# First feed-forward of a two-block transformer kernel: 512-column products with halves added on VectorE, and a re-timed plan

## The chip, the cores and the metric

One core of one Trainium2 chip runs the whole program. The metric is device time in microseconds (us) for one execution. Below, TensorE, VectorE, ScalarE and GpSimd appear in rows of the profile as PE, DVE, ACT and POOL; SPq is the queue from which the weight loads are issued.

## What is computed

Two transformer blocks, one after the other, on one sequence of 256 tokens of width 1024, in float32. The first block has a mixer of three branches (a forgetting attention, a gated delta rule, a stick-breaking attention), a memory cross-attention, and the feed-forward that this change is about. The second block has a feed-forward, a mixer (blockwise attention with 8 heads beside a pooling mixer), a memory cross-attention and another feed-forward. The feed-forward of the first block has a causal convolution of three taps over the tokens between its two products:

```
def conv_ffn(h, w_up, conv_w, conv_b, w_down):
    u = causal_dwconv(h @ w_up, conv_w) + conv_b
    a, b = jnp.split(u, 2, axis=-1)
    return (jax.nn.silu(a) * b) @ w_down
```

`w_up` is 1024 x 5632, `w_down` 2816 x 1024. The other two feed-forwards are `(silu(h @ w_gate) * (h @ w_up)) @ w_down` of the same sizes, without convolution.

## The kernel before

**Chunks.** All weights stream through once in chunks of 1 MB, on a ring of three slots (`RING = 3`). A chunk is loaded to `raw`, ScalarE rounds it to the high part `whi` (step `hi`, line 1443), and VectorE forms the low part `wlo = raw - whi` (step `lo`, line 1693). The activations are split in the same way (`xh` and `xl`, side by side in `xhl`), and each product is the sum of three: high by high, high by low, low by high. `hi` of a chunk waits until the product three chunks before has ended; the load of a chunk waits for the `lo` three chunks before. `hi` and `lo` are issued two chunks ahead (`LEAD = 2`).

**Kinds of chunk.** Kind A (line 1131) multiplies in three matmuls of 256 columns for each of 8 k-blocks and 2 column blocks: 48 matmuls, and all three sums land in the same 256 columns of one PSUM bank. Kind W (lines 1139 and 1142) multiplies `whi` once with `xh` and `xl` joined (512 columns) and `wlo` with `xh` (256 columns): 32 matmuls, two banks, and the two halves of each bank have to be added afterwards, which VectorE does with a TENSOR_REDUCE (steps `add`, `ga`, `ua`). Kinds V (line 1158) and R (line 1170) have the activations as the stationary side; R is the kind of the down and output products, with 4 banks, 24 matmuls a chunk.

**Order of the work.** `build_plan` writes one list of steps; each engine runs its own steps of the list strictly in that order. For each chunk `c`, `mm(c)` puts down `hi(c+2)` and `lo(c+2)`, then what was left over in the list `late`, then the product in two halves, and then the steps that read it. Between the halves and between chunks `hook` lets "links" of side chains in (the heads of the attentions, the norms): a link goes in when the planner's own clock, advanced by the cost table `ROUGH`, says that its input has been done for long enough (`fits`, with `EARLY` and `EARLY_LONG`). The real waits are semaphore waits; the planner's clock only decides the place of the link in the order. Side chains are not present in the feed-forwards.

**First feed-forward, before.** 11 pairs of chunks (gate `g`, up `u`), both of kind A. After the pair's second product: `ca(i)` on ScalarE (line 1644: last tap times the product plus bias, four instructions, read from the banks), `cd(i)` on VectorE (line 1950: the two other taps, eight instructions, read from the banks). In the next pair's first chunk, behind `hi` and `lo` of that chunk: `fs` (ScalarE, silu), `fm` (VectorE, line 1984), `fh` (ScalarE, line 1662), `fl` (VectorE, line 1988). So VectorE's order in a pair is lo, fm, fl, lo, cd, and ScalarE's hi, fs, fh, hi, ca. 11 chunks of `w_down` (kind R) follow. The other two feed-forwards have kind W and steps `ga(i)` after the gate product and `ua(i)` after the up product (lines 1975 and 1980).

**Second block's mixer, before.** The four pooling windows are made by GpSimd (`pl_win`), multiplied by TensorE (`pl_mm`, line 1417) in the middle of the fourth chunk before `w_out_2`, into banks 2 and 3, and read by `pl_h` (ScalarE) and `pl_l` (VectorE). The first R chunk of `w_out_2` waits for the last readers of all four of its banks before its first matmul.

## Time and profile before

| | |
|---|---|
| median of 3 runs | 1211.7 us (1209.04 to 1212.9) |
| the profiled execution | 1205.77 us |
| its span | 1204.0 us |
| granted TensorE clock, mean | 0.991 of full |
| TensorE busy | 1156.5 us, 96% |
| VectorE busy | 811.0 us, 67% |
| ScalarE busy | 614.9 us, 51% |
| GpSimd busy | 80.9 us, 7% |
| chain that ended last | TensorE 85%, VectorE 7%, ScalarE 4% |
| products of the first feed-forward's up stage | from about 443 to 569.7 us of the span |

The profile is of one execution on the hardware. The busy time of an engine counts its instructions alone; a matmul's end is modelled and overlaps the next one, so that the distance between starts tells the pace and not the duration of one. "Idle before" with a releaser is how long an engine stood before an instruction and what ended the wait.

### The profile page before, as it was taken

The numbers are of one execution on the slowest core, as the hardware profiler recorded it, in microseconds if no ns is written. First come the engines' busy times: TensorE is split into PE (matmuls) and PEld (weight loads), VectorE is DVE, ScalarE is ACT, GpSimd is POOL, SyncE is SP. The second block draws the span as 40 slices with busy tenths as digits, with TensorE's granted clock in tenths as the row PEclk, the third lists the DMA queues.
The fourth block names the chain that finished last, engine by engine and source line by source line (L and its number), as shares of the span: only waits on it lengthen the run. The fifth ranks groups of instructions, "written<-read, shape, count | busy, mean of one in ns | idle before, by whom it ended". The sixth has DMA issues, their size and how long they took to land.

```text
span 1204.0 us, 16670 instructions
## 1 busy us (share of the span) xinstructions
PE 1156.5 (96%) x6747; PEld 1005.7 (84%) x6747; DVE 811.0 (67%) x865; ACT 614.9 (51%) x780; POOL 80.9 (7%) x114
## 2 busy tenths in 40 slices
PE   6999999999998899999999999999999997999997
PEld 6878988888987789999888888888776886888886
DVE  6877565855778667787647777647666656777743
ACT  6556344434767556555436444436345546444442
POOL 8001100200000000000000000002700000000000
PEclk9999999999999999999999999999999998999999
DMA  8644332433565336555665656555443524666550
GB/s 255 189 143 138 105 106 82 130 105 105 210 210 173 108 104 202 191 188 176 210 197 166 197 177 202 182 201 182 167 140 105 178 85 142 191 192 192 181 203 36
DMA packets 144132, 193.95 MB, mean 161 GB/s; under 512 B 6136, under 2 KB 121208, under 8 KB 144056
## 3 DMA queue, kind: packets, MB, share of 16 engines
q1 hardware_dynamic: 142856, 188.43, 48.1%
q0 software_dynamic: 1200, 4.46, 1.0%
q8 instruction: 54, 0.88, 0.3%
q14 instruction: 22, 0.18, 0.0%
HBM read 191.82 MB, written 1.05 MB: 160 GB/s over the span
## 4 chain that ended last, share of the span: by engine, by line
PE 85%; DVE 7%; ACT 4%; issue 2%; DMA 1%; SPq 0%; ACTq 0%; DVEq 0%
PE banks L1139 23%; PE banks L1170 19%; PE banks L1131 13%; PE banks L1142 11%; PE banks L1158 5%; DVE wlo L1693 2%; PE banks L1149 2%; ACT whi L1443 2%; PE banks L1383 1%; PE banks L1184 1%; PE banks L1214 1%; PE banks L1303 1%; PE banks L1257 1%; PE banks L1266 1%; DMA raw<-in_w_in 1%
## 5 line engine op out<-in xcount | busy, mean ns | idle before, releaser
L1693 DVE TENSOR_TENSOR wlo<-raw,whi 128x2048 fp32r<-128x2048 f32 x178 | 407.4, 2292 | 187.7 <-ACT whi L1443 187.6
L1443 ACT ACTIVATE whi<-raw 128x2048 fp32r<-128x2048 f32 x178 | 339.4, 1910 | 182.2 <-PE banks L1170 88.5
L1139 PE MATMUL banks<-xhl,whi 128*128 128x512 f32 x1248 | 403.9, 405 | 3.4 <-DVE fq_ L1968 1.6
L1142 PEld LDWEIGHTS banks<-xhl,wlo 128*128 128x128 f32 x1248 | 235.7, 189 | 55.8
L1142 PE MATMUL banks<-xhl,wlo 128*128 128x256 f32 x1248 | 246.9, 279 | 0.0
L1139 PEld LDWEIGHTS banks<-xhl,whi 128*128 128x128 f32 x1248 | 192.6, 190 | 11.8 <-issue 6.9
L1131 PE MATMUL banks<-xhl,whi 128*128 128x256 f32 x912 | 165.0, 284 | 0.0
L1131 PEld LDWEIGHTS banks<-xhl,whi 128*128 128x128 f32 x912 | 142.1, 192 | 0.5 <-DVE xhl L1708 0.2
L1131 PE MATMUL banks<-xhl,wlo 128*128 128x256 f32 x456 | 129.0, 283 | 0.0
L1170 PE MATMUL banks<-whi,hh 128*128 128x512 f32 x264 | 102.7, 389 | 0.0
L1170 PE MATMUL banks<-wlo,hh 128*128 128x512 f32 x264 | 102.7, 389 | 0.0
L1170 PE MATMUL banks<-whi,hl 128*128 128x512 f32 x264 | 102.7, 389 | 0.0
L1131 PEld LDWEIGHTS banks<-xhl,wlo 128*128 128x128 f32 x456 | 87.5, 192 | 0.0
L1662 ACT ACTIVATE hh<-SG 128x512 fp32r<-128x512 f32 x33 | 20.9, 632 | 93.0 <-DVE SG L1984 93.0
L1170 PEld LDWEIGHTS banks<-whi,hl 128*128 128x128 f32 x264 | 49.6, 188 | 10.4
L1170 PEld LDWEIGHTS banks<-whi,hh 128*128 128x128 f32 x264 | 49.6, 188 | 10.1
L1170 PEld LDWEIGHTS banks<-wlo,hh 128*128 128x128 f32 x264 | 49.6, 188 | 10.1
L1980 DVE TENSOR_REDUCE CA<-banks 128x512 f32<-128x1024 f32 x22 | 27.0, 1225 | 25.9 <-PE banks L1142 25.9
L1950 DVE SCALAR_TENSOR_TENSOR CA<-banks,pcol,CA 128x255 f32<-128x255 f32 (+1 forms) x88 | 36.4, 476 | 8.4 <-ACT CA L1644 8.0
L1988 DVE TENSOR_TENSOR hl<-SG,hh 128x512 fp32r<-128x512 f32 x33 | 22.9, 693 | 27.3 <-ACT hh L1662 27.3
L1158 PE MATMUL banks<-whi,xhl 128*128 128x512 f32 x96 | 35.1, 422 | 0.0
L1708 DVE SCALAR_TENSOR_TENSOR xhl<-banks,pcol,xhl 128x256 fp32r<-128x256 f32 x56 | 24.2, 479 | 8.8 <-ACT xhl L1472 8.7
(354 smaller groups left out, 1505.5 us busy)
## 6 DMA issues: line engine op xcount, KB each, us to landing
raw<-in_w_in SPq DMA_DIRECT2D x40, 1024.0 KB, 5.3
raw<-in_w_up SPq DMA_DIRECT2D x22, 1024.0 KB, 5.1
raw<-in_ffn_w_gate SPq DMA_DIRECT2D x22, 1024.0 KB, 5.3
raw<-in_ffn_w_up SPq DMA_DIRECT2D x22, 1024.0 KB, 5.3
raw<-in_ffn_w_down SPq DMA_DIRECT2D x22, 1024.0 KB, 5.0
raw<-in_w_down SPq DMA_DIRECT2D x11, 1024.0 KB, 5.0
raw<-in_w_out SPq DMA_DIRECT2D x8, 1024.0 KB, 5.1
raw<-in_xa_wkv SPq DMA_DIRECT2D x8, 1024.0 KB, 5.4
```

The source lines that it names most:

```text
L1131: ins = pe.matmul(o, a[:, k, cols_], v[:, k, :], start=(k == 0 and i == 0), stop=(k == KD - 1 and i == 2))
L1139: pe.matmul(bank(b[m]), wh[:, k, m * P:(m + 1) * P], both[:, k, :, :].rearrange("p a t -> p (a t)"), start=(k == 0), stop=(k == KD - 1), s ...
L1142: ins = pe.matmul(bank(b[m])[:, 0:T], wl[:, k, m * P:(m + 1) * P], Xh[:, k, :], start=False, stop=(k == KD - 1), skip_group_check=True)
L1149: ins = pe.matmul(bank(b[part])[:, m * T:(m + 1) * T], a[:, k, o:o + P], v[:, k, :], start=(k == 0 and i == 0), stop=(k == NH - 1 and i == 2))
L1158: ins = pe.matmul(bank(b[t]), v[:, k, t * P:(t + 1) * P], a[:, kk, :], start=(k == 0 and i == 0), stop=(k == KD - 1 and i == 2))
L1170: ins = pe.matmul(bank(b[2 * t + nb]), v[:, k, t * P:(t + 1) * P], a[:, kk, nb * 512:(nb + 1) * 512], start=(ch["first"] and kk == 0 and i ...
L1443: act.activation(whi[c % RING][:, :], raw[c % RING][:, :], ACT.Copy).then_inc(act_done, 1)
L1693: dve.tensor_tensor(wlo[c % RING][:, :], raw[c % RING][:, :], whi[c % RING][:, :], ALU.subtract).then_inc(dve_done, 1)
L1708: dve.scalar_tensor_tensor(l_[:, k, :], turned(name, k), pcolumn(name, k), h_[:, k, :], ALU.mult, ALU.subtract).then_inc(dve_done, 1)
L1950: ins = dve.scalar_tensor_tensor(d, bank(chunks[c]["banks"][0])[:, m * T:(m + 1) * T - s], pcolumn("ffn_conv", (2 - s) * 2 * KF + a * KF + ...
L1980: dve.tensor_reduce(mat(CA[i % 2][:, 1, :]), halves(c), AX_X, ALU.add).then_inc(dve_done, 1)
L1988: dve.tensor_tensor(hl[:, 2 * i:2 * i + 2, :], mat(SG[i % 2]), hh[:, 2 * i:2 * i + 2, :], ALU.subtract).then_inc(dve_done, 1)
```

## The change

In words: the 22 chunks of the first feed-forward's up stage become kind W (`wide`), on banks 4(left mod 2) and up. A new SBUF tile `FS` of 2 x 512 elements takes the sums: `ga(0, i)` adds the halves of the gate product into it, `ua(0, i)` those of the up product. `ca(i)` and `cd(i)` read `FS` in place of the banks; both go to `late`, that is into the next pair, between `lo` of its first chunk and `fs`. VectorE's order in a pair becomes lo, cd, fm, fl, ga, lo, ua, and ScalarE's hi, ca, fs, fh, hi. Beside this: the cost table gets costs by kind of attention and by kind of chunk, `EARLY` and `EARLY_LONG` change, a link that begins on another engine than TensorE is also measured by that engine's clock, `hi` is also held behind the estimated load; the turn of the second memory's norm is held until the sum before it; the eight heads of the blockwise attention are chained in two groups a lane; the pooled products go one chunk sooner and into banks 0 and 1; `w_out_2` takes its banks in the order 2, 3, 0, 1; and an R chunk waits for the readers of a half's banks just before that half.

```diff
@@ -25,7 +25,7 @@
 RING = 3
-EARLY, EARLY_LONG = 0.2, 0.8
+EARLY, EARLY_LONG = 0.5, 0.6
 LEAD = 2
@@ -73,7 +73,14 @@
          "g_bc": 0.9, "g_egc": 0.63, "g_qg": 0.6, "r_ws": 0.9, "r_vn": 0.6, "r_o": 1.8, "r_oc": 0.35, "r_s": 1.1,
-         "sc": 1.3, "sm": 1.4, "ex": 0.85, "pn": 0.8, "pt": 0.7, "pc": 0.5, "pv": 0.7, "oc": 0.4, "ol": 0.45,
+         ("sc", "fox"): 1.3, ("sm", "fox"): 1.25, ("ex", "fox"): 0.9, ("pn", "fox"): 0.85, ("pt", "fox"): 0.67,
...
+         ("sc", "moba"): 0.65, ("sm", "moba"): 1.5, ("ex", "moba"): 0.95, ("pn", "moba"): 0.85, ("pt", "moba"): 0.67,
...
@@ -97,7 +104,7 @@
         elif name == "hi" and ("mm", args[0] - RING, 1) in self.ended:
-            behind = self.ended["mm", args[0] - RING, 1]
+            behind = max(self.ended["mm", args[0] - RING, 1], self.ended["lo", args[0] - RING] + 5.8)
         elif engine == "pe" and name in ("mm", "mma"):
@@ -105,12 +112,12 @@
         if name == "ns" and args[0] == "mem_g_2":
-            behind = self.ended["nd", "norm_mem", 1] + 9.0
+            behind = self.ended["nd", "norm_mem", 1] + 11.0
         if name == "nl":
             behind = max(end_ for key_, end_ in self.ended.items() if key_[0] == "nh")
-        cost = ROUGH.get(name, 0.3)
+        cost = ROUGH.get(name, ROUGH.get((name, *args[:1]), 0.3))
         if name in ("mm", "mma"):
-            cost = 0.7 if self.chunks[args[0]]["kind"] == "S" else 2.83
+            cost = {"S": 0.8, "A": 2.88, "O": 2.88, "W": 2.82, "V": 2.74, "R": 2.74}[self.chunks[args[0]]["kind"]]
             if name == "mma" or ("mma", *args) in self.ended:
@@ -159,7 +166,7 @@
                             srcs=[((0, 1024), kpn(w[name][256 * j:256 * j + 256, :]))],
-                            x=x, banks=tuple(range(base, base + 4)), evac=evac if nth == n - 1 else None, name=name))
+                            x=x, banks=base if type(base) is tuple else tuple(range(base, base + 4)), evac=evac if nth == n - 1 else None, name=name))
@@ -206,9 +213,9 @@
             if f == 0:
-                b = 2 * (left % 4)
-                cols(gate, 256 * i, "x", (b,), None, f=f, i=i, part="gate")
-                cols(up, c_up + 256 * i, "x", (b + 1,), "ffn", f=f, i=i, part="up")
+                b = 4 * (left % 2)
+                wide(gate, 256 * i, "x", "sum", (b, b + 1), f=f, i=i, part="gate")
+                wide(up, c_up + 256 * i, "x", "ffn", (b + 2, b + 3), f=f, i=i, part="up")
             else:
@@ -228,7 +235,7 @@
         wide(win, 256 * i, "x", "add", to="qk", i=i)
-    rows("w_out_2", 4, "y5", "post", 0, (2, 3, 0, 1))
+    rows("w_out_2", 4, "y5", "post", (2, 3, 0, 1), (2, 3, 0, 1))
     xa_v(1, (4, 5))
@@ -273,6 +280,9 @@
                 ready_ = max(ready_, input_of(s))
+        first_ = "pe" if callable(link_[0]) else link_[0][0]
+        if first_ != "pe":
+            return ready_ <= max(pl.clock["pe"], pl.clock[first_]) + EARLY
         return ready_ <= pl.clock["pe"] + (EARLY if chain is not long_ else EARLY_LONG)
@@ -323,7 +333,7 @@
             if "f" in ch:
-                reader = ("cd", ch["i"]) if ch["f"] == 0 else ("ua" if ch["part"] == "up" else "ga", ch["f"], ch["i"])
+                reader = ("ua" if ch["part"] == "up" else "ga", ch["f"], ch["i"])
             else:
@@ -362,6 +372,8 @@
             pl.add("dve", "add", c)
+        elif ev == "sum":
+            pl.add("dve", "ga", ch["f"], ch["i"])
         elif ev == "gate":
@@ -379,8 +391,8 @@
             if f == 0:
-                pl.add("act", "ca", i)
-                pl.add("dve", "cd", i)
+                pl.add("dve", "ua", f, i)
+                late.extend([("act", "ca", i), ("dve", "cd", i)])
             rest = [("dve", "fm", f, i), ("act", "fh", f, i), ("dve", "fl", f, i)]
@@ -574,7 +586,7 @@
     side.append(turn_m2)
-    finished[id(turn_m2)] = pl.ended["nd", "mem_g_2", 1]
+    finished[id(turn_m2)] = max(pl.ended["nd", "mem_g_2", 1], pl.ended["add", c - 1])
     mm(c)
@@ -614,13 +626,13 @@
     for lane in range(2):
-        side.append(heads_of("moba", [lane, lane + 2, lane + 4, lane + 6]))
-    for _ in range(3):
-        mm(c)
-        c += 1
-    pl.take(("pl_mm",), (2, 3), ("pl_l",))
-    mm(c, mid=[("pe", "pl_mm"), ("act", "pl_h"), ("dve", "pl_l")])
-    c += 1
+        side.append(heads_of("moba", [lane, lane + 2]) + heads_of("moba", [lane + 4, lane + 6]))
+    mm(c)
+    mm(c + 1)
+    pl.take(("pl_mm",), (0, 1), ("pl_l",))
+    mm(c + 2, mid=[("pe", "pl_mm"), ("act", "pl_h"), ("dve", "pl_l")])
+    mm(c + 3)
+    c += 4
     for j in range(2):
@@ -759,6 +771,7 @@
         CA = [sb(f"CA{i}", [P, 2, 512], stack=r3) for i in range(2)]
+        FS = sb("FS", [P, 2, 512], stack=r3)
         SG = [sb(f"SG{i}", [P, 512], stack=r3) for i in range(2)]
@@ -785,7 +798,7 @@
-            return bank(2 + g % 2)[:, (g // 2) * T:(g // 2 + 1) * T]
+            return bank(g % 2)[:, (g // 2) * T:(g // 2 + 1) * T]
@@ -1111,7 +1124,7 @@
                         pe.wait_ge(DONE[plan.engine[step[0]]], at(*step))
-                for t in () if 0 not in quarters else (part, 1) if ch["kind"] == "R" and part == 0 else (part,):
+                for t in () if ch["kind"] == "R" or 0 not in quarters else (part,):
                     for step in plan.bank_wait.get(("mm", c, t), []):
@@ -1163,6 +1176,8 @@
                         t, q = (part, half) if ch["last"] else (half, part)
+                        for step in plan.bank_wait.get(("mm", c, half), []) if part == 0 else []:
+                            pe.wait_ge(DONE[plan.engine[step[0]]], at(*step))
                         for kk in (0, 1) if ch["last"] else (q,):
@@ -1634,14 +1649,13 @@
-                cg, cu = pair(0, i)
-                act.wait_ge(pe_done, at("mm", cu, 1))
+                act.wait_ge(dve_done, at("ua", 0, i))
                 if i >= 2:
                     act.wait_ge(dve_done, at("fm", 0, i - 2))
-                for a, c in enumerate((cg, cu)):
+                for a in range(2):
                     for m in range(2):
                         f = a * KF + 2 * i + m
-                        ins = act.activation(CA[i % 2][:, a, m * T:(m + 1) * T], bank(chunks[c]["banks"][0])[:, m * T:(m + 1) * T],
+                        ins = act.activation(CA[i % 2][:, a, m * T:(m + 1) * T], FS[:, a, m * T:(m + 1) * T],
                                              ACT.Identity, scale=pcolumn("ffn_conv", 2 * 2 * KF + f), bias=pcolumn("ffn_conv_b", f))
@@ -1944,10 +1958,10 @@
                 for s in (1, 2):
-                    for a, c in enumerate(pair(0, i)):
+                    for a in range(2):
                         for m in range(2):
                             d = CA[i % 2][:, a, m * T + s:(m + 1) * T]
-                            ins = dve.scalar_tensor_tensor(d, bank(chunks[c]["banks"][0])[:, m * T:(m + 1) * T - s],
+                            ins = dve.scalar_tensor_tensor(d, FS[:, a, m * T:(m + 1) * T - s],
                                                            pcolumn("ffn_conv", (2 - s) * 2 * KF + a * KF + 2 * i + m), d,
@@ -1970,14 +1984,14 @@
                 dve.wait_ge(pe_done, at("mm", c, 1))
-                if i >= 2:
+                if f and i >= 2:
                     dve.wait_ge(act_done, at("fs", f, i - 2))
-                dve.tensor_reduce(mat(CA[i % 2][:, 0, :]), halves(c), AX_X, ALU.add).then_inc(dve_done, 1)
+                dve.tensor_reduce(mat(CA[i % 2][:, 0, :] if f else FS[:, 0, :]), halves(c), AX_X, ALU.add).then_inc(dve_done, 1)
                 dve.wait_ge(pe_done, at("mm", c, 1))
-                dve.tensor_reduce(mat(CA[i % 2][:, 1, :]), halves(c), AX_X, ALU.add).then_inc(dve_done, 1)
+                dve.tensor_reduce(mat(CA[i % 2][:, 1, :] if f else FS[:, 1, :]), halves(c), AX_X, ALU.add).then_inc(dve_done, 1)
```

## Rows read from the trace of the kernel before

**Rows 1.** The page's busy time, share of the span and instructions.

```profile
PE 1156.5 (96%) x6747; PEld 1005.7 (84%) x6747; DVE 811.0 (67%) x865; ACT 614.9 (51%) x780; POOL 80.9 (7%) x114
```

**Rows 2.** Stretches: first and second up stage; length, busy PE, PEld, DVE, ACT, POOL, clock.

```profile
449.00:576.00 127.00, 127.00 (x1036) 125.92 (x1035) 99.54 (x131) 75.03 (x88) 0.00 (x0) 1.00 0.58 191
652.00:776.00 124.00, 124.00 (x694) 107.52 (x693) 90.88 (x65) 55.77 (x45) 0.00 (x0) 1.00 0.60 193
```

**Rows 3.** Timeline of TensorE and load queue; last, loads' issues, us to landing.

```profile
544.90 0.40 PE L1131 MATMUL banks<-xhl,whi 128*128 128x256 f32 x2
...
545.26 0.40 PE L1131 MATMUL banks<-xhl,whi 128*128 128x256 f32 x2
...
644.36 0.63 PE L1139 MATMUL banks<-xhl,whi 128*128 128x512 f32 x2
...
649.94 0.63 PE L1139 MATMUL banks<-xhl,whi 128*128 128x512 f32 x2
...
606.94 0.37 SPq L954 DMA_DIRECT2D raw<-in_xa_wkv  x1
612.38 0.37 SPq L954 DMA_DIRECT2D raw<-in_ffn_w_gate  x1
...
raw<-in_w_up SPq DMA_DIRECT2D x22, 1024.0 KB, 5.1
```

**Rows 4.** Timeline of VectorE and ScalarE in the first feed-forward.

```profile
446.35 6.71 DVE L1693 TENSOR_TENSOR wlo<-raw,whi 128x2048 fp32r<-128x2048 f32 x3
...
460.10 2.28 DVE L1693 TENSOR_TENSOR wlo<-raw,whi 128x2048 fp32r<-128x2048 f32 x1
462.42 0.69 DVE L1984 TENSOR_TENSOR SG<-SG,CA 128x512 f32<-128x512 f32 x1
463.94 0.69 DVE L1988 TENSOR_TENSOR hl<-SG,hh 128x512 fp32r<-128x512 f32 x1 [0.83 <-ACT hh L1662]
...
468.36 3.34 DVE L1950 SCALAR_TENSOR_TENSOR CA<-banks,pcol,CA 128x255 f32<-128x255 f32 x8 [0.39 <-ACT CA L1644]
...
460.26 1.28 ACT L1654 ACT_TABLE_LOAD   x1 [1.72 <-DVE CA L1950]
...
466.33 1.93 ACT L1644 ACTIVATE CA<-banks,pcol 128x256 f32<-128x256 f32 x4 [0.68 <-PE banks L1131]
468.14 1.92 ACT L1443 ACTIVATE whi<-raw 128x2048 fp32r<-128x2048 f32 x1
```

**Rows 5.** Groups with shapes apart: busy us, mean ns of one, idle before.

```profile
L1980 DVE TENSOR_REDUCE CA<-banks 128x512 f32<-128x1024 f32 x22 | 27.0, 1225 | 25.9 <-PE banks L1142 25.9
L1794 DVE SCALAR_TENSOR_TENSOR gM<-gM,gcols,strict 128x128 f32<-128x128 f32 x8 | 2.3, 348 | 0.1
L1834 DVE SCALAR_TENSOR_TENSOR gS<-gS,gX,banks 128x128 f32<-128x128 f32 x16 | 4.5, 344 | 7.5 <-PE banks L1305 7.5
L1575 ACT ACTIVATE S<-banks,small 128x256 f32<-128x256 f32 x16 | 7.4, 470 | 17.9 <-DVE small L1857 17.8
L1575 ACT ACTIVATE S<-S,small 128x256 f32<-128x256 f32 x12 | 5.9, 493 | 0.0
```

**Rows 6.** TensorE's timeline: rows with a wait outside the first feed-forward.

```profile
385.13 2.72 PE L1184 MATMUL banks<-ident,xs 128*128 128x128 f32 x16 [2.71 <-DVE mq_ L1968]
...
865.85 0.55 PE L1361 MATMUL banks<-ident,S 128*128 128x128 f32 x3 [2.57 <-DVE S L1865]
...
892.49 0.47 PE L1170 MATMUL banks<-whi,y5h 128*128 128x512 f32 x1 [2.17 <-DVE qk_ L1968]
```

**Rows 7.** Stretches around such waits; the eighth number is the granted clock.

```profile
383.00:391.00 8.00, 5.87 (x26) 4.92 (x27) 7.29 (x11) 4.78 (x10) 0.00 (x0) 0.79 0.68 236
...
868.00:872.00 4.00, 4.00 (x14) 2.78 (x13) 1.06 (x4) 3.14 (x6) 0.00 (x0) 0.65 0.00 0
890.00:898.00 8.00, 5.83 (x34) 4.43 (x33) 5.37 (x8) 2.89 (x3) 0.00 (x0) 1.00 0.52 182
```

**Rows 8.** Timeline of GpSimd: the last instruction of the pooling windows.

```profile
865.52 0.85 POOL L1087 TENSOR_TENSOR pin<-win,pin 128x256 f32<-128x256 f32 x1
```

6 rows, old and new, of the table ROUGH are left out of this document.

## The prediction

> **What bounds the kernel now.** I read the page's busy times first [rows 1]: TensorE is busy for 1156.5 of 1204.0 us, 96%. Over the whole span it is the bound, and only 47.5 us of its time are idle. The second view is the table of stretches [rows 2], because an average hides what a stage does: in the first feed-forward's up stage VectorE is busy 99.5 of 127 us (78%), in the second's 90.9 of 124 us. TensorE has no idle time in either. The third view is the timeline of the stage. Of kind A one k-block and column block takes 0.36 us (544.90 to 545.26), a chunk 16 x 0.36 = 5.76 us, a pair 11.52 us; of kind W one k-block takes 5.58/8 = 0.697 us (644.36 to 649.94), a chunk 5.57 us, a pair 11.14 us; a chunk of kind R takes 5.44 us, the distance of two loads in steady state [rows 3]. The fourth is the order on VectorE in that stage with its waits [rows 4].
>
> **Part 1, TensorE's work.** 22 chunks become 0.19 us shorter: -4.2 us, if TensorE stays the bound.
>
> **Part 2, VectorE's work.** Added: two sums of halves a pair at 1.225 us, the duration of the same instruction in the other feed-forwards [rows 5]: 22 x 1.225 = 27.0 us. VectorE's 99.5 us of this stage become 126.5, more than the 22 x 5.57 = 122.5 us of TensorE, before any wait is counted. The order adds waits. A pair on VectorE is now lo 2.29, cd 3.35, a wait for fs, fm 0.69, a wait for fh, fl 0.69, ga 1.23, lo 2.29, ua 1.23. The waits for fs and fh each hold one ScalarE instruction of 0.64 us and two handoffs, 0.78 us; the trace shows 0.83 for the one it has [rows 4]. Before, a `lo` stood between cd and fm and hid fs; now nothing does. Instructions in a row overlap by up to 0.09 us (468.36 + 3.34 against a next start at 471.62), so I take no more for handoffs: 11.79 us of work and 2 x 0.78 of waits, **13.35 us a pair** against TensorE's 11.14.
>
> What else could wait, and doesn't: ScalarE has hi 1.92 twice, ca 1.93 (four instructions), fs and fh 0.64 each, 7 us a pair; ca runs beside the lo ahead of cd, hi of the up chunk beside fl and ga. The single tile FS adds no wait, since ga(i) stands behind cd(i-1), its last reader, on the same engine. The banks are those of the pair before last, long read. Loads keep up: two of 5.1 us a pair [rows 3]. Behind the late VectorE stand `lo`, so TensorE waits there, and SP's next load.
>
> cd and ca read SBUF now. For VectorE the trace has the same operation with an operand in PSUM at 344 ns and from SBUF alone at 348 ns (128 columns) [rows 5], so cd stays 3.35 us; 0.4 us either way is its bound. For ScalarE it is 470 against 493 ns [rows 5], so ca becomes some 2.03 us, hidden behind lo.
>
> **The sum for the stage.** VectorE's first `lo` of the stage runs until 453 or so (three in a row from 446.35, sums in between), ua(0) starts at 454.4. The next pair holds the silu table load, 1.28 us, and a wait of 0.7 for hi, so ua(1) is at 454.4 + 13.35 + 1.98 = 469.7. Nine more pairs: ua(10) at 589.9. Behind it stand ua 1.23, lo 2.29, cd 3.35, 0.78, fm 0.70, then fh until 0.71 later, hi 1.92, lo 2.29 and two handoffs of 0.07 before the fourth chunk of `w_down` can start: 603.2. In the trace `w_down` starts at 569.7 (the last of 22 x 5.76 us of products from 443.0), its fourth chunk at 569.7 + 3 x 5.44 = 586.1. Behind it `w_down` is bound by TensorE, 5.44 us a chunk against 2.29 of VectorE, and gives nothing back. **+17.1 us**, the 4.2 already in it. Seen from TensorE: waits of 2.2 us at the up chunk of each pair from the fifth on, about 1 us at the fourth's, and two of 2.3 to 2.4 in `w_down`: 21.2 us idle, less 4.2. Bounds: cd at 0.4 less or more a pair moves this by 4.4; 0.05 more at each of three handoffs, by 1.7. So +11 to +23.
>
> A rule bears on cd. In the trace SBUF and PSUM sources cost the same [rows 5]. The Trainium skill (VectorE: DVE Perf Modes, section on the TRN2 errata) gives a fixed part of 58 cycles from SBUF and 120 from PSUM at 0.96 GHz; eight instructions would each be 65 ns shorter, and the stage's sum, an estimate, +11.4 instead of +17.1.
>
> **Part 3, the plan elsewhere.** Three waits are named by the edits [rows 6]. (a) `w_out_2` waits 2.17 us for the sum into banks 0 and 1; with the order 2, 3, 0, 1 its first half needs banks 2 and 3 only. The pooled products now sit in banks 0 and 1 one chunk earlier, and the chunk behind must wait for pl_l: 0 to 1 us back. -2. On GpSimd nothing moves; its windows end at 866.4 [rows 8], and the products now stand near 880 (1.5 chunks, themselves and a link before the wait at 890.3), so they don't wait for it. (b) The turn of the second memory waits 2.71 us for a sum on VectorE, and the clock is 0.79 over the 8 us around it, 1.7 us lost [rows 6, 7]. Held back until that sum, it should cost neither: -4.4 if the turn lands right, I take -3. (c) The first head pair of the blockwise attention waits 2.57 us for its probabilities, and the clock is 0.65 over 4 us behind it, 1.4 us [rows 6, 7]. New costs and the two groups a lane move these links: between -4 and +1, I take -1.5. The other links, placed by 0.3 us earlier or 0.2 later than before: -3 to +3, I take -0.5. Sum **-7**, bounds -13 to +4; no row shows a link's new place, so this is the loose term.
>
> Total: +17.1 - 7 = **+10**. The profiled execution would go from 1205.8 to 1215.8 us; it stands 5.9 us under the median, so against the median 1211.7 + 10 = 1221.7 us.
>
> **Rivals.**
> 1. *Forecast*, 0.64: VectorE is the bound in the up stage, part of it is returned elsewhere. 1221.7, its own range 1215 to 1228.
> 2. *The plan gives nothing back*, 0.18: new waits replace those removed, or the waits of 2.2 us bring the clock to its lower level of 1.2 GHz. Waits of 2.57 and 2.71 had such a spell behind them, one of 2.17 had none [rows 6, 7]. Within a pair a spell of 1.7 us is covered (11.14 + 1.7 < 13.35); in `w_down` two would cost 3.4. 1211.7 + 17 + 0 to 4: about 1230.
> 3. *Faster, by the plan*, 0.07. The place is the links outside the feed-forwards; the price is what is left of the 47.5 us of idle time [rows 1] and of the slow spells. It decides once more than 17 us come back. The three named waits and their clock give 10.6, so every other wait would have to go too. With 22 us back: 1207.
> 4. *VectorE's reads from SBUF are cheaper*, 0.09: cd at 2.83 us, stage +11.4, total +4.4: 1216. Against it the 344 and 348 ns [rows 5].
> 5. *Two SBUF sources are slower*, 0.02. If each of the eight instructions took twice its 255 columns' time, 0.27 us more, cd would be 5.45 us, a pair 15.5, the stage +40: 1245. The rows have such an instruction at 348 ns for 128 columns, which leaves no room [rows 5]. The Trainium skill (Vector Engine (DVE) Microarchitecture Reference, Points that are easy to get wrong) says that this shape with two sources in SBUF that are not bf16 halves throughput; by that rule this rival would hold.
>
> That the change does not do what it says would need FS to be unused; its steps are plain in the diff, and I give that no chance of its own.
>
> **The numbers.** 1221.7 is the likeliest case's. The range 1210 to 1233 takes in the bounds of the stage (+11 to +23) with the middle of the plan's term, rival 4 and most of rival 2, and leaves out rivals 3 and 5. 0.3% of this kernel, 3.6 us, is about what a measurement can tell from no change. Faster by over that: rival 3, 0.07. Within it: the low end of rivals 1 and 4, 0.06. Slower: 0.87.
>
> **What would show it.** Right: VectorE over 90% busy from 470 to 600 us, L1950 at 3.35 us for eight with no wait ahead, a wait of 0.8 before both L1984 and L1988; TensorE at L1139 waiting for wlo L1693 some seven times by 2.2 us in the up stage, twice in `w_down`; pairs 13.35 us apart; the first R chunk of `w_out_2` without its wait; the turn at 385 without 2.7. Wrong: pairs 11.14 us apart (VectorE is not the bound), or L1950 far from 474 ns.

## The result and the profile after

The changed kernel takes 1219.99 us (median of 5 runs, 1218.37 to 1221.68), the kernel before 1209.38 us (5 runs, 1205.07 to 1212.9). The ratio is 1.0086, 95% interval 1.0062 to 1.0109: slower by 10.6 us. Forecast were +10 us and 1221.7 us. The two profiled executions are farther apart: spans 1218.2 and 1204.0 us, +14.2. The profiled execution of before (1205.77 us) lay at the low end of its runs; e5 below shows where two executions of one kernel can differ.

The page of the changed kernel has these busy times (engines: busy us, share of the span, instructions), to be read beside [rows 1]:

```profile
PE 1158.1 (95%) x6395; PEld 989.5 (81%) x6395; DVE 836.6 (69%) x887; ACT 616.2 (51%) x780; POOL 82.3 (7%) x114
```

TensorE's work hardly changes, VectorE's rises by 25.6 us. The stretch that holds the up stage, from the table of stretches of the changed kernel (length; busy PE, PEld, DVE, ACT, POOL; granted clock), answers to the first row of [rows 2]:

```profile
449.00:591.00 142.00, 127.63 (x695) 109.35 (x694) 119.15 (x143) 74.24 (x83) 0.00 (x0) 0.98 0.49 160
```

TensorE has 14.4 us without work where it had none, and VectorE is busy for 119.2 of 142 us, 84%. VectorE's timeline in a pair of that stage shows the chain, from one `ua` to the next:

```profile
496.79 1.23 DVE L1994 TENSOR_REDUCE FS<-banks 128x512 f32<-128x1024 f32 x1
497.93 2.28 DVE L1707 TENSOR_TENSOR wlo<-raw,whi 128x2048 fp32r<-128x2048 f32 x1
500.28 3.37 DVE L1964 SCALAR_TENSOR_TENSOR CA<-FS,pcol,CA 128x255 f32<-128x255 f32 x8
504.50 0.69 DVE L1998 TENSOR_TENSOR SG<-SG,CA 128x512 f32<-128x512 f32 x1 [0.85 <-ACT SG L1668]
506.02 0.69 DVE L2002 TENSOR_TENSOR hl<-SG,hh 128x512 fp32r<-128x512 f32 x1 [0.83 <-ACT hh L1676]
506.75 1.22 DVE L1989 TENSOR_REDUCE FS<-banks 128x512 f32<-128x1024 f32 x1
507.89 2.28 DVE L1707 TENSOR_TENSOR wlo<-raw,whi 128x2048 fp32r<-128x2048 f32 x1
510.20 1.23 DVE L1994 TENSOR_REDUCE FS<-banks 128x512 f32<-128x1024 f32 x1
```

From 496.79 to 510.20 are 13.41 us. The only gaps are the two waits for ScalarE of 0.85 and 0.83, and no instruction waits for a product. TensorE's waits from the norm's turn to the end of `w_down` (waiting engine and line, releaser; total us, times, longest):

```profile
PE banks L1152 <- DVE wlo L1707: 13.8, 8, 2.4
PE banks L1152 <- DVE xhl L1722: 2.9, 1, 2.9
PE banks L1185 <- DVE wlo L1707: 2.7, 2, 2.1
```

Two of these I had priced; the one of 2.9 us for xhl I had not. It stands ahead of the first product of the stage in TensorE's timeline; a wait of the common kind, and the last of the kind in `w_down`, are beside it:

```profile
442.69 0.70 PE L1152 MATMUL banks<-xhl,whi 128*128 128x512 f32 x2 [2.94 <-DVE xhl L1722]
...
510.22 0.73 PE L1152 MATMUL banks<-xhl,whi 128*128 128x512 f32 x2 [1.98 <-DVE wlo L1707]
...
604.02 0.50 PE L1185 MATMUL banks<-whi,hh 128*128 128x512 f32 x1 [2.13 <-DVE wlo L1707]
```

To see where time goes and comes from, I cut every profiled execution at two places that can be found in TensorE's timeline: the first transpose of the norm ahead of the first feed-forward, and the first product behind `w_down` (`xa_k(3)`). "Ahead" is from the span's start to the first, "feed-forward" between them, "behind" from the second to the end.

| kernel | ahead | feed-forward | behind | span | median of runs |
|---|---|---|---|---|---|
| before | 440.3 | 189.3 | 574.4 | 1204.0 | 1209.4 to 1211.7 |
| changed | 437.7 | 211.6 | 568.9 | 1218.2 | 1220.0 |
| e1, the feed-forward's part alone | 440.2 | 211.6 | 575.7 | 1227.5 | 1229.5 |
| e2, the plan's part alone | 436.1 | 189.3 | 570.8 | 1196.2 | 1197.9 |
| e3, other banks for the first pair | 440.7 | 209.4 | 570.9 | 1221.0 | 1217.3 |
| e4, other order | 438.1 | 194.6 | 569.2 | 1201.9 | 1203.3 |
| e5, before again | 442.5 | 189.3 | 578.6 | 1210.4 | one run |
| e6, fl on GpSimd | 437.7 | 190.9 | 568.0 | 1196.6 | 1199.3 |
| e7, one tap left out | 437.6 | 190.9 | 569.1 | 1197.6 | one run |
| e8, old turn | 439.8 | 189.3 | 568.0 | 1197.1 | 1199.6 |
| e9, gate A and up W | 436.7 | 195.4 | 571.1 | 1203.2 | 1203.5 |
| e10, e2 again | 441.0 | 189.3 | 568.0 | 1198.3 | 1199.9 |
| e11, old pooled products | 438.0 | 189.3 | 569.4 | 1196.7 | 1198.2 |
| e12, e9 with one bank changed | 437.7 | 187.3 | 568.1 | 1193.1 | 1196.1 |

The change costs 22.3 us between the cuts and gains 2.6 + 5.5 = 8.1 us outside.

Two things of the table have to be known before it is read. The profiled execution of e3 is the slowest of its six runs. And the column "ahead" holds a difference that comes from no kernel: in the stretch of TensorE's first chunk some executions run at half pace. Before, the changed kernel and e5, in this order:

```profile
14.00:18.00 4.00, 3.60 (x31) 3.63 (x32) 3.78 (x9) 3.75 (x5) 3.55 (x7) 1.00 0.97 294
14.00:18.00 4.00, 3.56 (x17) 3.59 (x18) 3.54 (x9) 3.51 (x5) 3.55 (x7) 1.00 0.97 300
14.00:18.00 4.00, 3.31 (x16) 3.34 (x17) 3.54 (x10) 3.48 (x6) 3.55 (x7) 1.00 0.91 280
```

In before, e1, e2, e6, e9 and e12 these 4 us hold 26 to 32 matmuls, in the other eight 16 to 19, although the granted clock of the rows is 1.00 in all of them; behind it those eight are 1.4 to 2.1 us later than the first profile of before, the changed kernel 1.6. It is chance and not the plan: e2 and e10 are the same kernel and stand on either side. Without it the changed kernel gains 4.2 us ahead, as e2 does.

### The profile page after: what moved, and what is told of

The parts are those of the page before. It is cut to its first block, busy times and chain, and to the rows that moved or that the text cites. A ratio compares the mean times of both kernels' runs of the same rounds, so it can differ in the third digit from the quotient of the medians.

```text
span 1218.2 us, 16005 instructions
## 1 busy us (share of the span) xinstructions
PE 1158.1 (95%) x6395; PEld 989.5 (81%) x6395; DVE 836.6 (69%) x887; ACT 616.2 (51%) x780; POOL 82.3 (7%) x114
## 4 chain that ended last, share of the span: by engine, by line
PE 75%; DVE 16%; ACT 5%; issue 2%; DMA 1%; DVEq 0%; ACTq 0%; SPq 0%
PE banks L1152 25%; PE banks L1185 18%; PE banks L1155 12%; DVE wlo L1707 6%; PE banks L1171 4%; PE banks L1144 3%; DVE CA L1964 3%; PE banks L1162 2%; ACT whi L1458 2%; PE banks L1398 1%; DVE FS L1994 1%; PE banks L1229 1%; DVE FS L1989 1%; PE banks L1272 1%; PE banks L1318 1%
## 5 line engine op out<-in xcount | busy, mean ns | idle before, releaser
L1152 PE MATMUL banks<-xhl,whi 128*128 128x512 f32 x1600 | 517.2, 405 | 20.2 <-DVE wlo L1707 14.6
L1155 PEld LDWEIGHTS banks<-xhl,wlo 128*128 128x128 f32 x1600 | 302.7, 189 | 71.9
L1155 PE MATMUL banks<-xhl,wlo 128*128 128x256 f32 x1600 | 316.7, 279 | 0.0
L1152 PEld LDWEIGHTS banks<-xhl,whi 128*128 128x128 f32 x1600 | 247.0, 190 | 30.5 <-DVE wlo L1707 16.4
L1185 PEld LDWEIGHTS banks<-whi,hh 128*128 128x128 f32 x264 | 50.0, 189 | 13.8 <-DVE wlo L1707 3.5
L1185 PEld LDWEIGHTS banks<-wlo,hh 128*128 128x128 f32 x264 | 49.9, 189 | 10.2
L1144 PE MATMUL banks<-xhl,whi 128*128 128x256 f32 x208 | 38.9, 290 | 0.0
L1964 DVE SCALAR_TENSOR_TENSOR CA<-FS,pcol,CA 128x255 f32<-128x255 f32 (+1 forms) x88 | 36.7, 479 | 1.5 <-DVE wlo L1707 0.4
L1144 PEld LDWEIGHTS banks<-xhl,whi 128*128 128x128 f32 x208 | 33.7, 199 | 0.0
L1658 ACT ACTIVATE CA<-FS,pcol 128x256 f32<-128x256 f32 x44 | 22.9, 591 | 19.9 <-issue 17.9
L1050 POOL TENSOR_TENSOR gMs<-gM,lev 128x512 f32<-128x512 f32 x12 | 21.3, 1775 | 138.4 <-DVE gM L1808 96.0
L1998 DVE TENSOR_TENSOR SG<-SG,CA 128x512 f32<-128x512 f32 x33 | 22.9, 693 | 11.3 <-ACT SG L1668 10.6
```

What stands on the lines that cost most here:

```text
L1144: ins = pe.matmul(o, a[:, k, cols_], v[:, k, :], start=(k == 0 and i == 0), stop=(k == KD - 1 and i == 2))
L1152: pe.matmul(bank(b[m]), wh[:, k, m * P:(m + 1) * P], both[:, k, :, :].rearrange("p a t -> p (a t)"), start=(k == 0), stop=(k == KD - 1), s ...
L1155: ins = pe.matmul(bank(b[m])[:, 0:T], wl[:, k, m * P:(m + 1) * P], Xh[:, k, :], start=False, stop=(k == KD - 1), skip_group_check=True)
L1185: ins = pe.matmul(bank(b[2 * t + nb]), v[:, k, t * P:(t + 1) * P], a[:, kk, nb * 512:(nb + 1) * 512], start=(ch["first"] and kk == 0 and i ...
L1658: ins = act.activation(CA[i % 2][:, a, m * T:(m + 1) * T], FS[:, a, m * T:(m + 1) * T], ACT.Identity, scale=pcolumn("ffn_conv", 2 * 2 * KF ...
L1964: ins = dve.scalar_tensor_tensor(d, FS[:, a, m * T:(m + 1) * T - s], pcolumn("ffn_conv", (2 - s) * 2 * KF + a * KF + 2 * i + m), d, ALU.mu ...
```

## The experiments

**e1 and e2 take the change apart.** e1 is the kernel before with the first hunk below and what belongs to it (FS, ca and cd from FS); e2 is the changed kernel with the same put back.

```diff
-                cols(gate, 256 * i, "x", (b,), None, f=f, i=i, part="gate")
-                cols(up, c_up + 256 * i, "x", (b + 1,), "ffn", f=f, i=i, part="up")
+                wide(gate, 256 * i, "x", "sum", (b, b + 1), f=f, i=i, part="gate")
+                wide(up, c_up + 256 * i, "x", "ffn", (b + 2, b + 3), f=f, i=i, part="up")
```

> The kernel before, with the first feed-forward's part of the change alone (kind W, FS, ga and ua, ca and cd from FS). Theory (VectorE is the bound of the up stage, and kind W also makes the first product wait for bank 0): VectorE's pairs 13.4 us apart as in the changed kernel, and 17 to 21 us slower than before. Rival (a good part of the loss comes from the rest of the plan): less than 14 us slower.

> The changed kernel with the first feed-forward put back to kind A, its sums from the banks and its old order; all of the rest of the change stays. Theory (the rest of the change returns time): faster than before by 6 to 9 us, with the wait at the second memory's turn and the one at w_out_2 gone. Rival (the rest returns nothing): within 2 us of before.

e1: 1229.5 us, ratio 1.0159 (1.0125 to 1.0194), 17.8 us over before's 1211.7 in the same series. Its feed-forward is 211.6 us long, to a tenth that of the changed kernel. So the whole loss is the feed-forward's own; the rest of the plan has no part in it. That the medians show 17.8 us and the stage 22.3 lies in the base: the profiled execution of before stands 3.6 to 5.9 us under the medians of before, that of e1 at its own median. e2: 1197.9 us, ratio 0.9894 (0.9871 to 0.9917), faster than before by 13.8 us, more than the 6 to 9 expected. In the profiled executions it gains 7.8 us, as expected. The excess is in the runs of before, and e5 goes after it.

**e3: the wait of 2.9 us is one for a bank.** The norm's transposes use banks 0 to 3 and the last column comes round to bank 0. The changed kernel's first gate product takes banks 0 and 1, so that its first matmul waits for the last `nl`; of kind A it took bank 4 and could begin behind the first column.

```diff
-                b = 4 * (left % 2)
+                b = 4 * (left % 2) if i else 4
```

> The changed kernel, but the first pair of the up stage uses banks 4 to 7 and not 0 to 3. Theory (the first W chunk waits 2.9 us for bank 0, which holds the last turned column of the norm, and VectorE's chain starts that much later): the wait ahead of the first product falls under 0.5 us, the whole kernel is 2 to 2.5 us faster than the changed one. Rival (the delay would have been swallowed by VectorE's backlog, which comes from its own work): less than 0.7 us.

TensorE's timeline in e3:

```profile
442.56 0.70 PE L1152 MATMUL banks<-xhl,whi 128*128 128x512 f32 x2
...
449.09 0.73 PE L1152 MATMUL banks<-xhl,whi 128*128 128x512 f32 x2 [0.72 <-DVE wlo L1707]
```

The transposes start at 440.7 and the products 1.8 us later, without a wait, where the changed kernel needs 5.0 us. The feed-forward is 2.2 us shorter (209.4 against 211.6). The time is 1217.3 us (ratio to before 1.0047, 1.0020 to 1.0073); the changed kernel was timed in another series, so the 2.7 us between the medians only fit. The theory holds: VectorE's chain starts with the first sums, so a late start is not swallowed by the backlog but carried through it.

**e4: the order of VectorE's steps.**

```diff
-                late.extend([("act", "ca", i), ("dve", "cd", i)])
+                late.extend([("act", "ca", i), ("dve", "cd", i, 0), ("act", "fs", f, i), ("dve", "cd", i, 1), ("dve", "fm", f, i)])
+                later.extend([("act", "fh", f, i), ("dve", "fl", f, i)])
```

`cd(i, 0)` does the gate's columns, `cd(i, 1)` the up columns; `later` is put down in the pair's second chunk, behind hi and lo.

> The changed kernel with the same instructions in another order: cd in two parts (gate columns, up columns) with fs beside the second; fm right behind; fh and fl behind hi and lo of the up chunk. VectorE has then no wait for ScalarE inside a pair. Theory (VectorE's 11.8 us of work and its two waits of 0.8 make the pair of 13.4): pairs 11.7 to 11.9 us apart, 14 to 18 us faster than the changed kernel. Rival (the work alone or contention sets the pace, the waits are covered): pairs still 13 us apart, less than 4 us faster.

1203.3 us, ratio 0.9934 (0.9911 to 0.9957): 16.7 us under the changed kernel's median, and faster than before. VectorE's timeline has no gap left:

```profile
519.67 2.28 DVE L1709 TENSOR_TENSOR wlo<-raw,whi 128x2048 fp32r<-128x2048 f32 x1
522.02 3.62 DVE L1966 SCALAR_TENSOR_TENSOR CA<-FS,pcol,CA 128x255 f32<-128x255 f32 x8
525.67 0.69 DVE L2000 TENSOR_TENSOR SG<-SG,CA 128x512 f32<-128x512 f32 x1
526.40 1.22 DVE L1991 TENSOR_REDUCE FS<-banks 128x512 f32<-128x1024 f32 x1
527.54 2.28 DVE L1709 TENSOR_TENSOR wlo<-raw,whi 128x2048 fp32r<-128x2048 f32 x1
529.86 0.69 DVE L2004 TENSOR_TENSOR hl<-SG,hh 128x512 fp32r<-128x512 f32 x1
530.59 1.22 DVE L1996 TENSOR_REDUCE FS<-banks 128x512 f32<-128x1024 f32 x1
531.73 2.28 DVE L1709 TENSOR_TENSOR wlo<-raw,whi 128x2048 fp32r<-128x2048 f32 x1
```

519.67 to 531.73 are 12.06 us: the two waits (1.68) are gone and cd in two parts costs 0.25 more (3.62 against 3.37). I had expected 11.7 to 11.9. Of the loss of 22.3 us, 17.0 came back with this order, 1.7 of them the half clock that the changed kernel has in `w_down` (below). e4 in turn has half clock behind its wait of 2.9 us ahead of the first product:

```profile
442.00:449.00 7.00, 5.99 (x18) 5.14 (x19) 6.54 (x6) 1.92 (x2) 0.67 (x2) 0.51 0.41 133
```

The pair is still bound by VectorE, 12.06 against 11.14.

**e7: VectorE's work, by taking some away.** The tap for two tokens back is left out, so half of cd's instructions and with them part of the convolution are missing.

```diff
-                for s in (1, 2):
+                for s in (1,):
```

> The changed kernel with the tap for two tokens back left out (four of cd's eight instructions), so that part of the convolution is missing. Theory (VectorE's chain sets the pace): pairs shorter by the 1.7 us of those four, 11.7 to 11.8 us apart, the time 15 to 17 us below the changed kernel's. Rival (TensorE's wait comes from something else, such as the loads or hi): less than 5 us.

VectorE's timeline, two successive `lo` ahead of cd:

```profile
527.53 2.28 DVE L1707 TENSOR_TENSOR wlo<-raw,whi 128x2048 fp32r<-128x2048 f32 x1
529.89 1.67 DVE L1964 SCALAR_TENSOR_TENSOR CA<-FS,pcol,CA 128x255 f32<-128x255 f32 x4
...
539.25 2.28 DVE L1707 TENSOR_TENSOR wlo<-raw,whi 128x2048 fp32r<-128x2048 f32 x1
```

Pairs are 11.72 us apart, 1.69 less than 13.41; the four instructions left out took 1.70 (1.67 against 3.37). The feed-forward is 20.7 us shorter, the span 20.6, more than the 15 to 17 expected: eleven pairs count (18.7), and the half clock in `w_down` (1.7) went too. The pair loses what VectorE's work loses, so VectorE is the bound.

**e6: fl on GpSimd**, in all three feed-forwards, on top of e4's order and e3's banks.

```diff
-            def fl(f, i):
-                dve.wait_ge(act_done, at("fh", f, i))
-                dve.tensor_tensor(hl[:, 2 * i:2 * i + 2, :], mat(SG[i % 2]), hh[:, 2 * i:2 * i + 2, :], ALU.subtract).then_inc(dve_done, 1)
+            def fl(f, i):
+                pool.wait_ge(act_done, at("fh", f, i))
+                pool.tensor_tensor(hl[:, 2 * i:2 * i + 2, :], mat(SG[i % 2]), hh[:, 2 * i:2 * i + 2, :], ALU.subtract).then_inc(pool_done, 1)
```

> e4's order and e3's banks, and fl (hl = SG - hh) on GpSimd, in all three feed-forwards. Theory (VectorE's work is the bound, 12.05 us a pair in e4 of which fl is 0.72): VectorE's pairs 11.3 us apart in the first feed-forward, the stage 6 to 9 us shorter than in e4, the time 1195 to 1199 us. Rival (GpSimd and VectorE hold each other up when both read SBUF): L1709's or the sums' durations rise above 2.3 and 1.23 us, pairs 11.8 or more, time 1200 or more.

1199.3 us, ratio 0.9923 (0.9891 to 0.9955), on the edge between the two. The timelines of VectorE and GpSimd decide for the rival:

```profile
522.14 3.14 DVE L1713 TENSOR_TENSOR wlo<-raw,whi 128x2048 fp32r<-128x2048 f32 x1
...
526.46 2.28 DVE L1713 TENSOR_TENSOR wlo<-raw,whi 128x2048 fp32r<-128x2048 f32 x1
...
534.33 3.14 DVE L1713 TENSOR_TENSOR wlo<-raw,whi 128x2048 fp32r<-128x2048 f32 x1
...
521.83 1.30 POOL L1093 TENSOR_TENSOR hl<-SG,hh 128x512 fp32r<-128x512 f32 x1 [10.88 <-ACT hh L1682]
```

GpSimd's 1.30 us instruction lies beside the `lo`, and that one takes 3.14 us where the next takes 2.28: 0.86 us lost for the 0.72 moved. Which of the two is held up depends on which began first. There GpSimd began 0.31 us ahead of the `lo`. In the first pair the `lo` began 0.66 us ahead, kept its 2.28 us, and GpSimd's instruction took 2.79, ending 1.17 us behind it:

```profile
462.07 2.28 DVE L1713 TENSOR_TENSOR wlo<-raw,whi 128x2048 fp32r<-128x2048 f32 x1
462.73 2.79 POOL L1093 TENSOR_TENSOR hl<-SG,hh 128x512 fp32r<-128x512 f32 x1 [18.92 <-ACT hh L1682]
```

The last pair of the stage shows the same (`lo` from 581.93 in 2.29 us, GpSimd from 582.76 in 2.62). Pairs are 12.19 us apart (522.14 to 534.33), longer than e4's 12.06. What e6 gains over e4 in this stage, 3.7 us, cannot be the move. 2.2 of it are e3's banks; e4's half clock at 442 to 449, which e6 does not have, costs up to 3.0; the longer pairs take some 1.4 back. The three nearly add up, but no run takes the half clock by itself.

**e5: why before's runs spread.**

> The kernel before, unchanged, for a second profile. Its runs spread over 7.5 us with a mean clock from 0.983 to 0.992, those of e2 over 2.1 us at 0.991 and 0.992. Theory (after its waits of 2.2 to 2.7 us TensorE's clock sometimes falls to half, and which waits do so changes from run to run; the new plan has removed those waits): this profile has more stretches at half clock than the first one had, behind the same waits, and its time is longer by about 1.7 us for each. Rival (the spread is in transfers or in the engines' work): the same stretches at half clock, and other waits are longer.

One execution of 1212.1 us, span 1210.4 against 1204.0. TensorE's waits are the same to a tenth (2.7 at the turn, 2.6 in the blockwise attention, 2.2 at `w_out_2`, 6.8 at the last norm). Nor are there more stretches at half clock, as I had expected: behind two of the waits the same stretch is longer. 12 us of each behind the blockwise attention's wait and from the end of the last norm's, first in the first profile of before, then in e5 (the eighth number is the clock):

```profile
866.00:878.00 12.00, 12.00 (x51) 9.12 (x51) 5.65 (x12) 6.28 (x14) 0.38 (x1) 0.86 0.22 75
1011.00:1023.00 12.00, 11.73 (x65) 10.67 (x66) 7.96 (x12) 7.93 (x11) 0.00 (x0) 0.87 0.21 63
```

```profile
868.00:880.00 12.00, 11.91 (x34) 8.44 (x35) 5.83 (x13) 4.76 (x11) 0.62 (x1) 0.57 0.17 47
1016.00:1028.00 12.00, 11.79 (x57) 10.69 (x58) 7.16 (x11) 6.59 (x10) 0.00 (x0) 0.74 0.21 61
```

In e5 the clock stays at its lower level, 1.2 GHz, for longer behind the same waits: 34 matmuls in 12 us where there were 51, and 57 where there were 65. In TensorE's timeline e5 needs 61.0 us from the first product behind the mixer norm to `w_out_2` where the first profile needs 58.4, and 127.25 against 125.83 from the last norm's transposes to the first product of the last `w_down`: 2.6 + 1.4 of the 6.4 us between the spans. Another 2.05 lie in the first chunk, which runs at half pace in e5 (the rows above). Only the 2.6 stand behind a wait that the change shortens (from 2.57 to 1.19 us). In the runs of before the clock goes with the time: beside e1 to e4 those of 1213 us and more have a mean clock of 0.983, the one of 1207.4 has 0.992; beside e5 it goes less closely (1213.1 us with 0.987). e2's are all at 0.991 or 0.992 and spread over 2.1 us (e10, the same kernel again, over 6.0 us with 0.989 to 0.993, so the spread does not go altogether). So a wait of some 2 to 3 us costs itself and can cost a stretch at half clock behind it, longer in some executions than in others. The plan's part of the change removed or shortened such waits, and gained 8 us against the profiled execution and 11 to 14 against the median. That the excess in the medians is the half clock behind those waits fits the clocks, but no run shows it.

**e8, e10 and e11: which part of the plan.** e8 is e2 with the turn as before; e11 is e2 with the pooled products, the bank order and the R chunks' waits as before; e10 is e2 again beside e9 and e11.

```diff
-    finished[id(turn_m2)] = max(pl.ended["nd", "mem_g_2", 1], pl.ended["add", c - 1])
+    finished[id(turn_m2)] = pl.ended["nd", "mem_g_2", 1]
```

```diff
-    rows("w_out_2", 4, "y5", "post", (2, 3, 0, 1), (2, 3, 0, 1))
+    rows("w_out_2", 4, "y5", "post", 0, (2, 3, 0, 1))
...
-    pl.take(("pl_mm",), (0, 1), ("pl_l",))
+    pl.take(("pl_mm",), (2, 3), ("pl_l",))
```

> e2 with one part put back: the turn of the second memory's norm may go in before the sum that it waits for, and its sum of squares 9 and not 11 us behind. Theory (this part alone gives back the wait of 2.7 us and a spell at half clock): the wait is there again, 3 to 5 us slower than e2. Rival (the other parts of the plan carry the gain): less than 1.5 us slower than e2.

> e2 again, beside e9 and e11 on one chip: 1197 to 1199 us, its runs within 3 us of one another.

> e2 with the pooled products back in the middle of the fourth chunk, in banks 2 and 3, the banks of w_out_2 in the order 0 to 3 and its first wait for all four. Theory (this part removes the wait of 2.17 us): the wait ahead of w_out_2 is back, 2 to 4 us slower than e10. Rival (the time was returned by the links' new places, which go with the costs): less than 1 us slower.

e8: 1199.6 us (ratio 0.9923, 0.9900 to 0.9947), against 1197.9 of e2 and 1199.9 of e10 (0.9921, 0.9902 to 0.9940; its runs lay within 6.0 us of one another, not 3). The wait is back, a row of TensorE's waits in e8:

```profile
PE banks L1199 <- DVE mq_ L1983: 2.7, 1, 2.7
```

and the stretch from the chunk ahead of the turn (381.9) to `xa_k(2)` (434.2) takes 52.3 us against 50.2 in e2 (380.3 to 430.5). So the turn is worth about 2 us, less than the 3 taken, and the medians cannot tell it: e8's lies 1.7 us above e2's, between the two expectations, and 0.3 under e10's. e11: 1198.2 us (0.9899, 0.9878 to 0.9920), not slower than e10. In its TensorE timeline the wait at `w_out_2` is

```profile
889.06 0.47 PE L1183 MATMUL banks<-whi,y5h 128*128 128x512 f32 x1 [0.79 <-DVE qk_ L1981]
```

0.8 us and not 2.17: with the new costs and the two groups a lane, the links have moved so that the sum comes earlier. From the first product behind the mixer norm to the end of `w_out_2`, e11 needs 88.7 us (831.8 to 920.5), e10 88.0 (834.8 to 922.8), before 94.0 (834.1 to 928.1, with 1.7 us lost to half clock). The rival holds: of the 6 us gained here, the pooled products' new place and the banks hold under 1, the links' places the rest.

**e9 and e12: a mixture.** If kind W pays only while VectorE's pair stays under TensorE's, half of it may pay. The gate chunk goes back to kind A and is read in its bank; the up chunk stays kind W; order as in e4.

```diff
-                wide(gate, 256 * i, "x", "sum", (b, b + 1), f=f, i=i, part="gate")
+                cols(gate, 256 * i, "x", (b if i else 5,), None, f=f, i=i, part="gate")
```

(e9 has `(b,)` there.)

> e4's order and e3's banks, with the gate chunks back in kind A (one bank, read there by ca and cd) and the up chunks alone in kind W through FS. VectorE has 10.8 us of work in a pair and TensorE 5.76 + 5.57 = 11.33. Theory (a kind W chunk pays only as long as VectorE's pair stays under TensorE's): no waits for wlo in the up stage, pairs 11.33 us apart, the stage 2.1 us shorter than e2's, the time 1195.5 to 1197. Rival (VectorE is late even so, or the order brings other waits): 1198 or more, with waits for wlo.

> e9 with the first pair's gate product in bank 5 and not 4, so that the second pair's gate does not wait for cd of the first. Theory (e9 lost 6.3 us to that wait and some 3.4 us to the half clock behind it, and its pairs of 11.33 us are the gain over e2): the wait is gone, the stage from the norm's turn to the end of w_down is 186 to 187.5 us long against 189.3 of the kernel before, the time 1194 to 1197 us. Rival (the clock or the loads take it back): 1198 or more.

e9: 1203.5 us (0.9948, 0.9932 to 0.9963), and not the 1195.5 to 1197 expected. Its pairs are 11.33 us apart, but one wait of TensorE was new:

```profile
PE banks L1146 <- DVE CA L1968: 6.3, 1, 6.3
```

The second pair's gate had the first pair's bank, and its reader is now cd, which comes late. e12 moves one bank: 1196.1 us (6 runs, 1194.8 to 1197.2), ratio 0.9893 (0.9868 to 0.9917). Its feed-forward is 8.1 us shorter than e9's: the wait of 6.3 and 1.8 for the half clock behind it, not the 3.4 that I gave that. TensorE has no wait left from the norm's turn to the end of `w_down`. The whole of it in the table of stretches, and VectorE's timeline from one pair to the next:

```profile
437.80:625.00 187.20, 187.18 (x1162) 168.42 (x1161) 150.41 (x165) 104.01 (x111) 0.67 (x2) 1.00 0.57 189
```

```profile
521.97 2.29 DVE L1710 TENSOR_TENSOR wlo<-raw,whi 128x2048 fp32r<-128x2048 f32 x1 [0.36 <-ACT whi L1460]
...
533.30 2.29 DVE L1710 TENSOR_TENSOR wlo<-raw,whi 128x2048 fp32r<-128x2048 f32 x1 [0.36 <-ACT whi L1460]
```

11.33 us a pair, now TensorE's pace, with VectorE waiting 0.36. The feed-forward takes 187.3 us, 2.0 under kind A's 189.3, which is the 11 x 0.19 us of the eleven shorter chunks. This is the fastest of the kernels run, 14.3 us under before in its series and about 24 under the changed kernel. Against e10 it is 3.8 us faster, against e2 1.8, over different series: that it beats the plan alone stands on the profile's 2.0 us, which nearly equal what the clock does to a run.

## Why the prediction was right, and where it was not

**VectorE becomes the bound of the up stage: right.** Pairs of 13.41 us against 13.35, the two waits 0.85 and 0.83 against 0.78, sums at 1.224 us. e4 (order) and e7 (work) each show it by itself, and e1 that nothing else is needed. One of my signs was wrong all the same, "VectorE over 90% busy from 470 to 600 us". It was not even in line with my own sum, 11.79 of 13.35 us or 88% (the terms listed for the 11.79 give 11.77), and the row has 111.2 of 130 us, 86%:

```profile
470.00:600.00 130.00, 115.63 (x614) 98.43 (x614) 111.21 (x138) 66.09 (x79) 0.00 (x0) 0.97 0.49 162
```

TensorE's long waits in the up stage were six of 1.98 to 2.35 us and not some seven of 2.2, and in `w_down` 0.6 and 2.13 and not two of 2.3 to 2.4.

**cd from SBUF costs the same: right.** The groups of the changed kernel for cd and ca:

```profile
L1964 DVE SCALAR_TENSOR_TENSOR CA<-FS,pcol,CA 128x255 f32<-128x255 f32 x44 | 18.4, 479 | 1.1 <-DVE wlo L1707 0.4
L1658 ACT ACTIVATE CA<-FS,pcol 128x256 f32<-128x256 f32 x44 | 22.9, 591 | 19.9 <-issue 17.9 <-DVE FS L1994 2.0
```

cd's instruction takes 479 ns from FS; from the banks it took 477 (the same shape in the trace of before). Rivals 4 and 5 fall with it. The Trainium skill (VectorE: DVE Perf Modes, the section on the TRN2 errata) would have it 65 ns shorter from SBUF, an estimate from its 58 and 120 cycles; this trace does not agree (479 against 477 ns). The Trainium skill (Vector Engine (DVE) Microarchitecture Reference, Points that are easy to get wrong) says that this shape with two SBUF sources that are not bf16 halves throughput; this trace does not agree either (479 against 477 ns). ca's instruction did grow, by 27 ns to 591, hidden as said.

**The sum for the stage, +17.1 us: too small by 5.2.** The fourth chunk of `w_down` was forecast for 603.2 and starts at 604.02; but the stage began 2.6 us earlier than before, and I had the same start. Three terms were missing or too small. (1) "The banks are those of the pair before last, long read" holds from the third pair on; for the first pair the readers are the norm's, and that cost 2.2 us (e3). (2) The half clock: behind TensorE's waits of 2.0 to 2.1 us it came three times in the feed-forward. Two rows of the stretches of the changed kernel show one inside a pair and one in `w_down`:

```profile
546.00:556.00 10.00, 8.01 (x37) 6.79 (x36) 9.55 (x10) 5.85 (x7) 0.00 (x0) 0.83 0.41 126
...
601.00:612.00 11.00, 8.87 (x32) 6.83 (x32) 6.79 (x3) 6.26 (x6) 0.00 (x0) 0.84 0.60 203
```

The first is covered, as worked out in rival 2: the next wait shrank from 1.99 to 0.43 us. The second is not: from that chunk to the end of `w_down` it took 45.26 us against 43.52, +1.7. (3) The pair is 0.06 longer than taken, 0.6 in all, and cd waited 0.4 once. Together 4.9 of the 5.2 us.

**The plan's part, -7 us: near in the profiled executions (-8.1, or -9.7 without the slow first chunk of the changed kernel), too small in the medians** (-10.6 and -13.8 by e10 and e2). Within the term, (b) the turn was 2 and not 3. (a), the wait of 2.17 us, went, but 1.4 of it with the links' new places and not with the banks (e11). (c), taken at -1.5, gave about 3: its wait fell from 2.57 to 1.19 us, and the half clock behind it, 1.7, is not there in the changed kernel. Of the 4.2 us ahead of the feed-forward, some 1.7 answer to a stretch at half clock that before, e1 and e5 have near 270 to 285 us and e3, e6 and e12 have too; whether the plan or chance took it away in the changed kernel stays open.

**The base: the weak step is "against the median 1211.7 + 10".** The sum was read from one execution of 1205.8 us and put on a median 5.9 us above it, without saying what the 5.9 us are. e5 shows what such a difference can be made of: 2.6 of its 6.4 us lie behind a wait that the change shortens, while 2.05 in the first chunk and 1.4 behind the last norm's wait of 6.8 us have nothing to do with the change. From the profiled execution the measured terms give 1205.8 + 22.3 - 8.1 = 1220.0.

So the total was right partly by luck: the base was 5.9 us too high and the stage 5.2 too low, and the two cancelled, with 1.1 from the plan. In the medians the account does not close: 17.8 us for the feed-forward (e1) less 10.6 to 13.8 for the plan (e10, e2) would be +4 to +7, and the change cost 10.6. The medians of before in the five series lie 2.3 us apart, which covers a part of that; the rest stays open. Rival 2 lent a piece (the half clock in `w_down`); rival 3, faster by the plan, needed 17 us and got at most 14.

## What to carry to other kernels

Before work is moved to an engine that is not the bound, sum that engine's work and its waits in one period of the stage, in the order in which it will run them: here 78% busy became 13.4 us of chain against 11.1, and three quarters of the loss (17.0 of 22.3 us) was order and not work. Look at the first and the last round of a rotation of banks by themselves, since their neighbours are others. And read several runs before one profile is taken as the base, and add terms read from a profile to that execution's own time: behind a wait of 2.6 us on TensorE the clock stayed at half for 10.2 us in one execution and for 3.4 in another, and the first chunk took some 2 us longer in eight of fourteen.

## What the runs showed of the hardware that was not expected

- Behind the same wait of 2.6 us on TensorE the clock stays at half for 3.4 us in one execution and for about 10 us in another (before and e5, the stretches above); of the changed kernel's six waits of 2.0 to 2.35 us in the up stage two had half clock behind them (those that ended at 550.5 and 577.3).
- TensorE's first chunk can run at half pace while the granted clock of the rows is 1.00 (17 matmuls against 31 in the same 4 us), in eight of fourteen profiled executions and with no tie to the kernel.
- When a GpSimd instruction of 1.30 us on SBUF begins 0.3 us ahead of a VectorE instruction that reads two SBUF tensors, that one goes from 2.28 to 3.14 us and GpSimd's keeps its 1.30; when VectorE's begins first, it keeps its 2.28 and GpSimd's takes 2.79 (e6). Neither slows both.
